# New latents of a two-layer encoder step: normalised and split by tokens instead of by chunks, with one sum moved on TensorE

## The reference

```python
h = rmsnorm(x, lp['norm_mix'])
proj = h @ lp['w_in']
u_pool, q_b, k_b, v_b, q_lat, kv_lat, kr_raw, gates = jnp.split(proj, IN_SPLITS, axis=-1)
cq = rmsnorm(q_lat, lp['mla_q_norm'])
c_kv = rmsnorm(kv_lat, lp['mla_kv_norm'])
k_rope = apply_rope(kr_raw, pos)
km, vm = mla_expand(c_kv, k_rope, lp['mla_w_kvup'], lp['mla_qk_k_norm'])   # keys, values of 8 heads
```

## Time and profile before

| what | value |
|---|---|
| median of three runs | 1045.93 us (1045.85 to 1046.44) |
| the profiled execution's own time | 1047.23 us |
| its span in the trace | 1045.3 us |
| PE busy | 1038.8 us, 99% |
| DVE busy | 641.6 us, 61% |
| ACT busy | 506.8 us, 48% |
| POOL busy | 314.3 us, 30% |
| chain that ended last, share of PE | 97% |
| mean granted clock of PE | 0.998 |

### The profile page before, as it was taken

How to read it: one execution, slowest core, us unless ns; L and a number is a source line. 1 busy time by engine, 2 the same in 40 slices (tenths; PEclk the granted TensorE clock), 3 DMA queues, 4 the chain that set the end, 5 groups by cost and what they waited for, 6 DMA issues and landing times.

```text
span 1045.3 us, 20059 instructions
## 1 busy us (share of the span) xinstructions
PE 1038.8 (99%) x7586; PEld 1005.6 (96%) x7586; DVE 641.6 (61%) x1079; ACT 506.8 (48%) x930; POOL 314.3 (30%) x277
## 2 busy tenths in 40 slices
PE   8999999999999999999999999999999999999998
PEld 6899999999999999999998999999999999999998
DVE  6888764445766666543567886554557565565443
ACT  6557755444554444434355585554445444433341
POOL 3365566541221111100133755656312211111000
PEclk9999999999999999999999999999999999999999
DMA  7455533244535544454514544333344354444441
GB/s 243 118 157 124 185 103 120 90 133 142 161 120 164 159 146 155 142 180 145 178 45 137 149 145 135 96 119 122 120 154 152 124 177 141 154 147 146 156 145 67
DMA packets 48707, 146.29 MB, mean 140 GB/s; under 512 B 8800, under 2 KB 14400, under 8 KB 48640
## 3 DMA queue, kind: packets, MB, share of 16 engines
q1 hardware_dynamic: 42416, 143.05, 44.3%
q10 hardware_dynamic: 6224, 2.30, 0.9%
HBM read 142.11 MB, written 3.22 MB: 139 GB/s over the span
## 4 chain that ended last, share of the span: by engine, by line
PE 97%; DVE 2%; DMA 0%; ACT 0%; issue 0%; SPq 0%; ACTq 0%
PE psum L566 29%; PE psum L567 28%; PE psum L568 28%; PE psum L739 1%; PE psum L778 1%; PE psum L761 1%; PE psum L721 1%; PE psum L722 1%; PE psum L726 1%; PE psum L769 1%; PE psum L698 1%; PE psum L811 1%; PE psum L994 0%; PE psum L866 0%; PE psum L693 0%; PE psum L694 0%
## 5 line engine op out<-in xcount | busy, mean ns | idle before, releaser
L566 PE MATMUL psum<-AH,WH 128*128 128x320 f32 x1328 | 414.4, 312 | 0.2
L568 PE MATMUL psum<-AH,WL 128*128 128x320 f32 x1328 | 410.3, 309 | 0.0
L567 PE MATMUL psum<-AL,WH 128*128 128x320 f32 x1328 | 410.2, 309 | 0.0
L566 PEld LDWEIGHTS psum<-AH,WH 128*128 128x128 f32 x1328 | 249.3, 188 | 7.3 <-issue 5.5
L567 PEld LDWEIGHTS psum<-AL,WH 128*128 128x128 f32 x1328 | 249.4, 188 | 0.2
L568 PEld LDWEIGHTS psum<-AH,WL 128*128 128x128 f32 x1328 | 249.3, 188 | 0.0
L1077 ACT CAST WH<-raw 128x1024 fp32r<-128x1024 f32 x166 | 172.7, 1046 | 129.2 <-PE psum L568 127.7
L1515 DVE TENSOR_TENSOR WL<-raw,WH 128x1024 fp32r<-128x1024 f32 x103 | 127.6, 1240 | 114.0 <-ACT WH L1077 113.6
L1978 POOL TENSOR_TENSOR WL<-raw,WH 128x1024 fp32r<-128x1024 f32 x60 | 147.6, 2478 | 114.7 <-ACT WH L1077 95.5
L1709 DVE TENSOR_TENSOR WL<-raw,WH 128x1024 fp32r<-128x1024 f32 x88 | 107.5, 1222 | 49.5 <-ACT WH L1250 48.2
L1983 POOL TENSOR_TENSOR fab<-fa,fb 128x320 f32<-128x320 f32 x44 | 38.6, 878 | 264.6 <-DVE fb L1714 264.6
(11 more groups left out here) (284 smaller groups left out, 1580.1 us busy)
## 6 DMA issues: line engine op xcount, KB each, us to landing
raw<-w_all SPq DMA_DIRECT2D x264, 512.0 KB, 3.5
y_out<-X SPq DMA_DIRECT2D x8, 160.0 KB, 2.7
X<-x_in SPq DMA_DIRECT2D x2, 320.0 KB, 5.7
X<-x_in SPq DMA_DIRECT2D x1, 640.0 KB, 7.4
lat_out<-ckv ACTq DMA_DIRECT2D x2, 320.0 KB, 2.9
scratch<-brel SPq DMA_DIRECT2D x8, 63.8 KB, 4.3
ckv<-lat_in SPq DMA_DIRECT2D x1, 384.0 KB, 5.5
bias<-scratch SPq DMA_DIRECT2D x8, 48.0 KB, 4.5
```

The lines of the kernel that those rows point to most:

```text
L566: mm(out, WH[:, slot, c0:c0 + cols], high, start=first, stop=False)
L567: mm(out, WH[:, slot, c0:c0 + cols], low, start=False, stop=False)
L568: return mm(out, WL[:, slot, c0:c0 + cols], high, start=False, stop=last)
```

## The change

The reciprocal, the normalisation, the cast and the subtraction of the new latents are cut by tokens, first 128 and then 192, each for both chunks together; before they were cut by chunks, each for all 320 tokens. The evacuation of the first query-latent tile stands inside the first part, that of the second inside the second part. The key block 4 now waits for the first part only (`ckv_ready` at `4 * l + 3`), the key block 5 for the second. In layer 0 `latent_sum` stands behind the second query-latent tile and not in its middle; layer 1 keeps its place.

```diff
@@ -670,14 +670,16 @@
-                pe.wait_ge(s.ckv_ready, 3 * l + 1)
+                pe.wait_ge(s.ckv_ready, 4 * l + 1)
             elif kb == 1:
                 pe.wait_ge(s.x_ready, 16 * l + 7)
-                pe.wait_ge(s.ckv_ready, 3 * l + 2)
+                pe.wait_ge(s.ckv_ready, 4 * l + 2)
             elif kb == CACHED:
                 pe.wait_ge(s.tile_free, l * NT + T_QL + 2)
-                pe.wait_ge(s.ckv_ready, 3 * l + 3)
-            elif kb != CACHED + 1:
+                pe.wait_ge(s.ckv_ready, 4 * l + 3)
+            elif kb == CACHED + 1:
+                pe.wait_ge(s.ckv_ready, 4 * l + 4)
+            else:
                 pe.wait_ge(s.kn_ready, l * KB + kb - 1)
@@ -923,7 +925,9 @@
-            dense(l, U_QL + 1, T_QL + 1, between=(lambda: latent_sum(l)) if l == 0 else None)
+            dense(l, U_QL + 1, T_QL + 1)
+            if l == 0:
+                latent_sum(l)
             turn_rope(l, 1)
@@ -1320,10 +1324,10 @@
+            act.wait_ge(s.ckv_first, l + 1)
+            nc.scalar.copy(ckvH[:, :, 0:128], ckv[:, :, 0:128]).then_inc(s.ckv_high, 1)
             act.wait_ge(s.stat_applied, l * NNORM + N_KV + 1)
-            nc.scalar.copy(ckvH[:, 0, 0:T], ckv[:, 0, 0:T]).then_inc(s.ckv_high, 1)
-            act.wait_ge(s.ckv_second, l + 1)
-            nc.scalar.copy(ckvH[:, 1, 0:T], ckv[:, 1, 0:T]).then_inc(s.ckv_high, 1)
+            nc.scalar.copy(ckvH[:, :, 128:T], ckv[:, :, 128:T]).then_inc(s.ckv_high, 1)
@@ -1774,15 +1778,16 @@
-            r = recip(l, N_KV, 128, T)
-            STT(ckv[:, 0, 0:T], kvr[:, 0, :], col(C_MKV, l), r, ALU.mult, ALU.mult).then_inc(s.stat_applied, 1)
-            STT(ckv[:, 1, 0:T], kvr[:, 1, :], col(C_MKV + 1, l), r, ALU.mult, ALU.mult).then_inc(s.ckv_second, 1)
-            scaled(l, T_QL, qlr[:, 0, :])
-            for c in range(2):
-                dve.wait_ge(s.ckv_high, 2 * l + c + 1)
-                ins = TT(ckvL[:, c, 0:T], ckv[:, c, 0:T], ckvH[:, c, 0:T].bitcast(F32), ALU.subtract)
-            ins.then_inc(s.ckv_ready, 1)
-            scaled(l, T_QL + 1, qlr[:, 1, :])
+            dve.wait_ge(s.std_ready, l * NSTAT + N_KV + 2)
+            for n, keys in enumerate((slice(0, 128), slice(128, T))):
+                r = stdk[:, N_KV % 2, keys]
+                link(l, v.reciprocal(r, r))
+                for c in range(2):
+                    ins = STT(ckv[:, c, keys], kvr[:, c, keys], col(C_MKV + c, l), r, ALU.mult, ALU.mult)
+                ins.then_inc(s.stat_applied if n else s.ckv_first, 1)
+                scaled(l, T_QL + n, qlr[:, n, :])
+                dve.wait_ge(s.ckv_high, 2 * l + n + 1)
+                TT(ckvL[:, :, keys], ckv[:, :, keys], ckvH[:, :, keys].bitcast(F32), ALU.subtract).then_inc(s.ckv_ready, 1)
             dve.wait_ge(s.both_high, l + 1)
```

4 lines of the change are left out of this document (2 added, 2 removed).

## The result

The change takes 1048.02 us (median of 18 runs, 1047.66 to 1049.08), the kernel before 1046.47 in the same rounds (18 runs, 1045.85 to 1047.89). The ratio is 1.0016 with a 95% interval of 1.0010 to 1.0022: slower, by about 1.7 us, with the interval on both sides of the 0.2% that the chances were drawn at. The forecast was 1048.0.

A forecast was written before the change was run, and what follows sets the result against it. The prediction took DVE to bound the stage in layer 0 and PE in layer 1, with no slack behind. Layer 0's 1.84 us plus layer 1's 0.20 made 2.04, taking the median from 1045.93 to 1048.0 us; range 1046.9 to 1049.8.

The forecast's parts named there:

- The bound: Latent stage: DVE bounds layer 0, where PE waits twice; PE bounds layer 1; no later slack absorbs a delay.
- the forecast's signs: Trace checks in layer 0: key block between 49.2 and 50.4, third evacuation at 51.6, latent sum at 43.1 to 43.2.
- Part 1, the sum: Layer 0: the later latent sum holds up DVE's reciprocal by 0.93 us; PE's gain there is worth nothing.
- Part 2, the cut: Layer 0: cutting by tokens lengthens DVE's chain from reciprocal to third evacuation, costing 0.91 us.
- The fixed latency per instruction: DVE: by a Trainium skill rule, three more instructions cost 0.47 us of the cut's 0.91.
- The key block: Layer 0: PE's key block starts 1.20 us later, at 49.81; needing only 128 tokens gives nothing.
- Layer 1: Third evacuation at 564.94 instead of 564.20; value block 0.09 later plus 0.11 for restarting, 0.20 us in all.
- The sum: Whole kernel: 1.84 us in layer 0 plus 0.20 in layer 1, 2.04 us slower, 1048.0; clock kept, 42%.
- The clock, the strongest rival: PE's idle time ahead of layer 0's key block drops the clock, losing 0.6 to 1.6 us: 1049.0; 40%.
- The rule on idle gaps: PE: a Trainium skill table warns of gaps longer than this one, so the clock stays and time is 1048.0.
- The cheaper chain: DVE's short products and reciprocals overlap more than priced: a cost of 1.2 to 1.4 us, 1047.2; 13%.
- The other side: Layer 0: the key block is held by the latent alone, PE stays the bound and the cut pays: 1044.5; 5%.

The follow-up runs named there:

- cut_only: The change with layer 0's latent sum back in the middle of the second query-latent tile, leaving the cut by tokens alone; 1047.26 us against 1046.31 before.
- evac_early: The change with the second query-latent tile's evacuation ahead of the second reciprocal, in both layers; 1050.18 us against 1046.31 before.
- split_last: The change with the third query-latent tile's evacuation ahead of the first pooling unit's weight split, in layer 0; 1048.72 us against 1046.31 before.
- sum_late: The kernel before with layer 0's latent sum moved behind the second query-latent tile, nothing else; 1047.12 us against 1046.31 before.
- delay_fixed: The change with two more reciprocals of 8 columns ahead of the first part, in layer 0; 1050.85 us against 1046.22 before.
- split_last_rope_first: `split_last` with POOL's split of the next unit behind its part of key block 4, in both layers; 1046.87 us against 1046.28 before.
- rearranged_chunks: The kernel before, cut by chunks kept, with later latent sum, `U_POOL` split on POOL, earlier rotary mean, POOL's next split later; 1050.14 us against 1046.28 before.
- ordered: `rearranged` with the `U_POOL` split back on DVE, in layer 0 behind key block 4's sum of squares; 1046.71 us against 1046.27 before.
- ordered_two_b: `ordered` with, in layer 0, ACT's second pooling cast between the latent casts and both splits on DVE behind key blocks 4 and 5; 1045.62 us against 1046.32.
- rearranged: The change with latent sum back inside the tile, earlier evacuations and rotary mean, `U_POOL` split on POOL, POOL's next split later; 1049.92 us against 1046.28 before.
- delay_short: The change with two more reciprocals of 160 columns ahead of the first part, in layer 0; 1051.60 us against 1046.28 before.

## Why the prediction was right, and where it was off

- **The bound: right.** DVE's queue ended PE's waits in layer 0 (`cut_only`, `evac_early` and `split_last` each moved a block with its evacuation), PE was the bound in layer 1, and no slack behind the stage took the delay up: the 1.57 us of layer 0 are still there at layer 1 (1.66) and at the end. In the times of the old trace (36.77 plus the time after the mark) the key block stands at 49.42 and the third evacuation at 51.37, inside the forecast's signs.
- **Part 1, the sum: right in kind, 0.13 too large.** It started at 41.80, 6.35 after the mark (the forecast's 43.15 is 6.38), and without an idle time. ACT's root came 0.74 behind it instead of 0.84, so the reciprocal was delayed by 0.80, not 0.93. The 0.84 was taken where dense matmuls follow the sum; now transposes do, and its row lasts 0.70 instead of 0.81. That a lighter neighbour is the reason was only argued. What PE gained at the sum was worth nothing, as said: `sum_late` makes it the whole difference, and is slower by 0.8 us.
- **Part 2, the cut: right in kind, 0.14 too large.** From the reciprocal to the third evacuation the forecast had 7.09, the trace has 6.95, before it was 6.18. By kind of instruction the 0.77 are: reciprocals 0.18, products 0.26, the longer way from the second evacuation to its subtraction 0.25 (0.18 of it the wait for the cast), first evacuation, subtractions and the rest 0.08. Single durations came out as worked out from the earlier trace rows: 0.95 and 1.35 for the reciprocals, 0.43 and 0.56 for the subtractions; the cast 0.51 as from the earlier trace rows. What was off is the time from start to start: 0.67 for the two products of 192 columns instead of 0.79, 0.34 for the first subtraction instead of 0.45. Two errors of opposite sign met here: up to the second evacuation the sum was 0.25 too large (4.72 against 4.47), behind it 0.11 too small (2.37 against 2.48), mostly since the second subtraction came 0.66 behind the second evacuation and not 0.56.
- **The fixed latency per instruction: agrees, and was no more than a part.** Three instructions more would be 0.47 us by the estimate from the Trainium skill, "VectorE: DVE Perf Modes", section on the TRN2 errata; `cut_only` shows 0.78 at the value block. `delay_fixed` measures such an instruction directly: 0.49 for two of eight columns.
- **The key block.** Forecast 1.20 later, measured 0.81, with a wait of 1.70 instead of 2.0, since part 1 was 0.13 too large and the cut up to the second evacuation 0.25. That the early half of the tokens buys nothing was right; `cut_only` has the key block at 11.86 against 11.84.
- **Layer 1: the mis-sized term.** 0.20 was added, of it 0.09 for the third evacuation and 0.11 for starting again. The evacuation came 0.60 later instead of 0.74, PE's start didn't move, and restarting cost 0.05, by the transposes 0.07. No wait shows there, though a short one was forecast.
- **The sum.** 2.04 was forecast; the traces give some 1.7, the ratio 1.67 (1.05 to 2.3). That 1048.0 was met to 0.02 us is in part luck: the median of three runs that it started from was 0.54 below the median of 18, and a sum 0.49 above the difference of the medians (1.55) made that good. The mis-sized terms are part 1, part 2 and layer 1, by 0.13 to 0.15 each.
- **The clock, the strongest rival.** It had 40% and didn't come with the change: 16 of 18 runs had a full mean clock, and the two at 0.998 (1048.75, 1049.08) are no more than the kernel before shows (4 of its 29 runs beside `sum_late` and `cut_only`). The change, `sum_late`, `split_last` and `split_last_rope_first` have an idle time of 1.68 to 1.72 us here, and none of their 51 runs was below 0.998. But the mechanism is real and near. With 0.49 us more of idle time four of five runs were below 1, three of them by more than a start explains; with 2.74 us five of six; with 3.21 three of six; with 4.09 all five. The traces show the fall behind the wait at 2.74 and 4.09, where it cost 1.7 and 0.4 us against the forecast's 0.6 to 1.6; at 2.19 and 3.21 only the mean clock speaks for it. No run was made at the 2.0 us of the forecast, so whether 40% was fair is open.
- **The rule on idle gaps.** By the Trainium skill, "TensorE: Matmul & The Clock Gate", in its table on why this matters, the clock stays at the change's gap, and its trace agrees: 1.00 from 48 to 60 us. By the same rule it would stay behind the 2.74 us of `rearranged_chunks`, and there it fell to 0.51: the measurement decides, and the rule is no margin to design by.
- **The cheaper chain.** At 6.95 the chain was nearer the forecast's 7.09 than this rival's, whose sum of 1.2 to 1.4 lies below the 1.57 of layer 0 alone.
- **The other side.** That the cut pays was given 5%, and in the change's order it doesn't. `ordered` and `ordered_two_b` show what it would have taken: with the second evacuation ahead of the second reciprocal, the third right behind its products and the weight split out of the way, the value block comes 1.08 us earlier with the cut than without.

## What to carry to other kernels

- A block that waits for its operand and for its bank starts at the later of the two. Making the operand earlier by cutting the work in front of it is worth something only if the bank's release moves too, and each instruction that a cut adds to a queue that is the bound costs (here 0.77 us for three).
- A term that the bounding engine waits for belongs early, even if the other engine then stands still for a moment: 0.24 us of idle time at the sum bought 0.80.
- A step that is taken out of one wait tends to land in the next queue (the weight split ahead of POOL's keys, the cast ahead of ACT's squares). Look at what each moved instruction is now ahead of, on every queue, before counting the gain.

## What the runs showed of the hardware

- **DVE waits for POOL on small things too.** The operation of three columns in SBUF (`krm`) took 0.60 us in the kernel before, 1.16 in the change and 1.48 in `split_last`, and 0.17 in `ordered`, where POOL was idle. In the first three it began during POOL's weight split and ended 0.02 to 0.03 behind it. From the timelines of the kernel before, the change and `ordered`:

```profile
51.79 0.60 DVE L1555 TENSOR_SCALAR krm<-krm 128x3 f32<-128x3 f32 x1
```

```profile
51.55 1.16 DVE L1559 TENSOR_SCALAR krm<-krm 128x3 f32<-128x3 f32 x1
```

```profile
49.85 0.17 DVE L1557 TENSOR_SCALAR krm<-krm 128x3 f32<-128x3 f32 x1
```

  It has one tensor input, and a table of costs by shape would never show it: its mean hides which neighbour it had. Giving POOL work because it is idle can cost DVE as much as the work was worth: in `rearranged` the split would have taken DVE 1.22 us, and one subtraction took 1.87 more.
- **Half a microsecond more of idle time may cost three.** With up to 1.72 us in one piece the clock stayed; at 2.19 us three of five runs were 2.5 to 3.9 us longer than the one with a full clock, most likely by this. Length alone doesn't order the cases: at 3.21 us three of six runs kept the full mean clock, though on another chip. How the idle time is spread may matter as well: 2.8 us in three pieces (`rearranged`) cost no clock in five runs.
- **A mean clock doesn't tell where, nor 1.00 that nothing was lost.** In three of the kernels profiled with a mean of 0.998 the loss lay within the first 12 us, before anything that was changed; only the windows told these from the falls behind the stage. In four more (`sum_late`, `ordered`, `delay_short`, `rearranged_chunks`) the windows say 1.00 for the start, and yet the matmuls of 512 columns start 0.43 us apart up to some 10 us, as they do in the stretch of `rearranged_chunks` that shows 0.51, where the change's start 0.23 apart. From the windows and PE's timeline of `sum_late`:

```profile
6.80:10.40 3.60, 3.58 (x9) 2.81 (x9) 2.45 (x2) 1.66 (x3) 0.00 (x0) 1.00 1.04 356
```

```profile
7.41 0.63 PE L694 MATMUL psum<-WKH,ckvL 128*128 128x512 f32 x1
7.84 0.63 PE L693 MATMUL psum<-WKH,ckvH 128*128 128x512 f32 x1
```

  The pace from one start to the next is the surer witness.
